# Hybrid decoder step: the last two prompt tiles' search moved into the block of the sample step

## The reference

```python
rel = relu(einsum('bthd,bsd->bths', iq, ik_all))      # 8 indexer heads of 64
score = einsum('bths,bth->bts', rel, iw)              # one score per query and key
score = where(k_pos <= q_pos, score, -inf)
_, sel = top_k(score, 256)
k_sel, v_sel = gather_kv(sel)                         # sample: from paged caches
p = softmax(q . k_sel * HEAD_DIM**-0.5 + rel_bias[bucket(q_pos - sel)])
o = p . v_sel
```

## Time and profile before

| | us |
|---|---|
| median of 3 runs | 4306.71 (4305.11 to 4307.8) |
| the profiled execution | 4302.77 |
| its span | 4301.3 |
| TensorE busy, share of the span | 3842.4, 89% |
| VectorE busy | 2194.8, 51% |
| ScalarE busy | 1531.6, 36% |
| GpSimd busy | 652.2, 15% |
| channels, first to last stores | about 205 to 1227 |
| block "step" | 1230 to about 1733 |

### The profile page before, as it was taken

How to read it: one execution, slowest core, us unless ns; L and a number is a source line. 1 busy time by engine, 2 the same in 40 slices (tenths; PEclk the granted TensorE clock), 3 DMA queues, 4 the chain that set the end, 5 groups by cost and what they waited for, 6 DMA issues and landing times. The chain is left out here.

```text
span 4301.3 us, 51935 instructions
## 1 busy us (share of the span) xinstructions
PE 3842.4 (89%) x19810; PEld 3139.1 (73%) x19882; DVE 2194.8 (51%) x4365; ACT 1531.6 (36%) x2446; POOL 652.2 (15%) x531
## 2 busy tenths in 40 slices
PE   7998887798859877888898879999999999989999
PEld 4554454455438556787887878899999999967877
DVE  6648988988963486343444333444434444430200
ACT  2135555665635334333333332322222222221211
POOL 0000000000000003322233210011111111133433
PEclk9999998999979669899999889999999999999999
DMA  3342222121142201111111124211211112163433
GB/s 113 94 99 56 73 49 61 46 63 39 47 145 94 80 9 45 32 37 28 48 36 45 33 78 132 79 40 40 59 39 55 44 39 59 47 227 108 137 114 107
DMA packets 287498, 298.52 MB, mean 69 GB/s; under 512 B 33871, under 2 KB 231375, under 8 KB 282410
## 3 DMA queue, kind: packets, MB, share of 16 engines
q1 hardware_dynamic: 264798, 250.51, 20.5%
q10 hardware_dynamic: 20400, 24.54, 1.7%
q0 software_dynamic: 2112, 20.97, 1.3%
HBM read 202.15 MB, written 94.10 MB: 69 GB/s over the span
## 5 line engine op out<-in xcount | busy, mean ns | idle before, releaser
L538 PE MATMUL chan_p_g<-ht,w_chan 128*128 128x412 f32 (+1 forms) x1760 | 677.2, 528 | 53.7 <-ACT chan_flat L586 33.6
L974 PE MATMUL up_p_g<-ht_high,up_wh 128*128 128x412 f32 (+1 forms) x1720 | 602.8, 350 | 0.0
L974 PE MATMUL up_p_g<-ht_high,up_wl 128*128 128x412 f32 (+1 forms) x1720 | 600.7, 349 | 0.0
L974 PE MATMUL up_p_g<-ht_low,up_wh 128*128 128x412 f32 (+1 forms) x1720 | 600.6, 349 | 0.0
L538 PEld LDWEIGHTS chan_p_g<-ht,w_chan 128*128 128x128 f32 x1760 | 341.4, 197 | 300.7 <-issue 233.5
L995 ACT ACTIVATE up_pre<-up_p_g 128x412 f32<-128x412 f32 (+1 forms) x220 | 113.2, 515 | 737.8 <-PE up_p_g L974 727.1
L1379 ACT ACTIVATE chan_signed<-chan_sc,chan_trial 128x512 bf16<-128x512 f32 (+6 forms) x224 | 304.9, 1361 | 148.4 <-DVE chan_trial L1434 127.7
L1059 DVE TENSOR_SCALAR up_acc<-up_pre,up_taps 128x2048 f32<-128x2048 f32 x44 | 59.3, 1347 | 557.8 <-ACT up_pre L995 557.8
L974 PEld LDWEIGHTS up_p_g<-ht_high,up_wh 128*128 128x128 f32 x1720 | 323.5, 188 | 1.1
L974 PEld LDWEIGHTS up_p_g<-ht_low,up_wh 128*128 128x128 f32 x1720 | 323.4, 188 | 1.2
L974 PEld LDWEIGHTS up_p_g<-ht_high,up_wl 128*128 128x128 f32 x1720 | 323.2, 188 | 0.5
(11 more groups left out here) (570 smaller groups left out, 7034.2 us busy)
## 6 DMA issues: line engine op xcount, KB each, us to landing
down_a<-scratch_act SPq DMA_DIRECT2D x88, 512.0 KB, 3.7
scratch_act<-up_acc SPq DMA_DIRECT2D x22, 1028.0 KB, 5.3
up_w<-in_w_up SPq DMA_DIRECT2D x44, 512.0 KB, 7.1
chan_iq<-scratch_iq SPq DMA_DIRECT2D x28, 512.0 KB, 7.3
scratch_qkv<-chan_acc SPq DMA_DIRECT2D x12, 1028.0 KB, 4.6
keys_of_raw<-scratch_qkv SPq DMA_DIRECT2D x16, 768.0 KB, 5.3
w_chan<-in_w_in SPq DMA_DIRECT2D x22, 512.0 KB, 4.6
proj_x<-in_x_prompt SPq DMA_DIRECT2D x16, 512.0 KB, 3.9
```

Of the source, the lines that this page charges most:

```text
L538: last = pe.matmul(p_g[u % BANKS][:, 0:cols.stop - cols.start], weights[:, k, :], K.ht[:, k, cols], start=(k == 0), stop=(k == KD - 1))
L974: last = pe.matmul(out, wp[s][:, k, :], hp[:, k, cols], start=(k == 0 and m == 0), stop=(k == KD - 1 and m == 2))
```

## The change

`Select` makes the scores of all pairs but searches only the first six (`self.searched`); its total shrinks by the last pair's search and masks. The scores of tiles 14 and 15 stay in SBUF (`K.last_sc`, held on the right side of SBUF until the end of "step"). A new class `LastSearch` runs their search and masks in the block "step", beside the attention, with one weight of 2.0 a round and 3.0 a mask (total 70); each engine advances it before the sample. The sample's index pages come in halves of a page (8 gathers instead of 4, each half as large, with buffers half as large), and the table's entries are loaded and doubled in channels. Values are gathered into the keys' buffer. ScalarE waits for the last sample score ahead of the rule.

```diff
@@ channels: sync, then vector
+            for req in range(2):
+                sp.dma_start(K.pid[req * NPAGE:(req + 1) * NPAGE, :], K.page_table[req], allow_slow_non_contiguous=True).then_inc(s_pid, 16)
...
+            dve.wait_ge(s_pid, 32)
+            dve.tensor_scalar(K.page_half[:, :, 0], K.pid[:, :], 1, None, ALU.logical_shift_left).then_inc(s_half, 1)
+            dve.tensor_scalar(K.page_half[:, :, 1], K.pid[:, :], 1, 1, ALU.logical_shift_left, ALU.bitwise_or).then_inc(s_half, 1)
+            dve.wait_ge(s_half, 2)
@@ Select
-        self.sc = two("sc", [P, SEQ])
+        self.sc = K.last_sc
+        self.searched = self.pairs[:-1]
...
-        return score + sum(32 * self.w_step(p) for p in self.pairs) + sum(self.w_mask(t) for _, _, t in self.tiles())
+        return score + sum(32 * self.w_step(p) + self.w_mask(2 * p) + self.w_mask(2 * p + 1) for p in self.searched)
...
+            if p not in self.searched:
+                return
@@ class LastSearch
+    W_COUNT, W_TRIAL, W_MASK = 1.0, 1.0, 3.0
...
+    def scalar(self, act):
+        for m in range(32):
+            act.wait_ge(self.s_tried, m + 1)
+            act.activation(self.signed[:, 0:self.NB], self.sc[1][:, 0:self.NB], ACT.Sign, scale=-1.0,
+                           bias=self.trial[:, 1:2].bitcast(F32), accum_out=self.signs[:, :]).then_inc(self.s_signs, 1)
+            yield self.W_COUNT
+            yield self.W_TRIAL
...
+    def vector(self, dve):
...
+            dve.wait_ge(self.s_tried, m + 1)
+            last = dve.tensor_scalar(self.tie[:, 0:self.NA], self.sc[0][:, 0:self.NA], trial[:, 0:1].bitcast(F32), None,
+                                     ALU.is_ge, ALU.add, accum_out=count[:, 0:1])
...
+            step(dve.tensor_scalar(miss[:, 0:1], count[:, 0:1], float(NSEL), None, ALU.is_lt))
+            yield self.W_COUNT
+            dve.wait_ge(self.s_signs, m + 1)
+            step(dve.tensor_scalar(miss[:, 1:2], self.signs[:, :], float(self.NB - 2 * NSEL), None, ALU.is_gt))
...
+            yield self.W_TRIAL
...
+            step(dve.tensor_scalar(tie, s, level, None, ALU.is_gt, ALU.add, accum_out=count[:, b:b + 1]))
+            dve.tensor_scalar(count[:, b:b + 1], count[:, b:b + 1], -1.0, float(NSEL), ALU.mult, ALU.add)
+            step(dve.tensor_scalar(tie, s, level, None, ALU.is_equal))
+            step(dve.tensor_scalar(left, s, level, None, ALU.is_lt))
+            step(dve.tensor_tensor_scan(s, tie, tie, 0.0, ALU.add, ALU.bypass))
+            step(dve.scalar_tensor_tensor(out=tie, in0=s, scalar=count[:, b:b + 1], in1=tie, op0=ALU.is_gt, op1=ALU.mult))
+            dve.tensor_tensor(left, left, tie, ALU.add).then_inc(self.s_left, 1)
+            yield self.W_MASK
@@ Sample
-        self.pages = [c.sb(f"pages{b}", [P, PAGE // 2, P]) for b in range(2)]
+        self.pages = [c.sb(f"pages{b}", [P, PAGE // 4, P]) for b in range(2)]
...
-        self.kg, self.vg = c.sb("kg", [P, QUARTERS, PAIRS, KVH * HD]), c.sb("vg", [P, QUARTERS, PAIRS, KVH * HD])
+        self.kg = c.sb("kg", [P, QUARTERS, PAIRS, KVH * HD])
+        self.vg = self.kg
...
-        cache = self.ins["cache_idx_k"].rearrange("l n p d -> (l n) (p d)")
+        cache = self.ins["cache_idx_k"].rearrange("l n (h p) d -> (l n h) (p d)", h=2)
...
     def begin(self, pool):
-        pool.wait_ge(self.S["pid"], 32)
...
         act.wait_ge(S["load"], 48)
+        act.wait_ge(S["sum"], self.UNITS)
@@ alongside, and its calls on SP, ScalarE and VectorE
-def alongside(main, side):
+def alongside(main, *sides):
     for w in main:
-        side.spend(w)
-    side.rest()
+        for side in sides:
+            side.spend(w)
+    for side in sides:
+        side.rest()
...
-                alongside(att.vector(dve), beside(sample.vector(dve)))
+                alongside(att.vector(dve), searching(last.vector(dve)), beside(sample.vector(dve)))
```

More of the change, by code:

```diff
@@ L458, in channels @@
         s_taps, s_zero, s_step, s_state, s_past = (c.sem(n) for n in ("taps", "zero", "step", "state", "past"))
+        s_pid, s_half = c.sem("pid"), c.sem("half")
         s_held, s_iqst = c.sems("held"), c.sems("iqst", IQS)
@@ L1341, in finished @@
     def finished(self, sp):
-        sp.wait_ge(self.s_out, 32 * len(self.pairs))
+        sp.wait_ge(self.s_out, 32 * len(self.searched))
     def tensor(self, pe):
@@ L2419, in __init__ @@
         self.S = {n: c.sem(f"s_{n}") for n in (
-            "pid iq wd bd w wread turn copy score mul sum "
+            "iq wd bd w wread turn copy score mul sum "
             "load state diag gates sq ss inv eg rs columns read vnew osq turned apart upd usum oss oinv ors mixed stored "
@@ L2555, in gpsimd @@
             yield self.W_SCORE
-            i = u // self.PER + 2
-            if (u + 1) % self.PER == 0 and i < PAIRS:
+            i = u // self.EACH + 2
+            if (u + 1) % self.EACH == 0 and i < self.HALVES:
                 pool.wait_ge(S["turn"], u + 1)
@@ L2660, in score_tensor @@
                 for k in range(4):
-                    last = pe.transpose(bank[u % 2][:, k * P:(k + 1) * P], self.pages[i % 2][:, u % self.PER * 4 + k, :], K.ident[:, :])
+                    last = pe.transpose(bank[u % 2][:, k * P:(k + 1) * P], self.pages[i % 2][:, u % self.EACH * 4 + k, :], K.ident[:, :])
                 last.then_inc(S["turn"], 1)
@@ L3175, in heads @@
             att = Attention(c, K, EARLY)
+            last = LastSearch(c, K)
             sample = Sample(c, K, ins, outs, bank)
             beside = lambda stream: Beside(stream, sample.total(), att.total())
+            searching = lambda stream: Beside(stream, last.total(), att.total())
             block = open_block(nc, stack, c)
@@ L3182, in _ @@
                 gate.sync(sp)
-                alongside(att.sync(sp, {-1: (0, 1), 6: (2,), 20: (3,)}), beside(sample.sync(sp)))
+                alongside(att.sync(sp, {-1: (0, 1), 6: (2,), 20: (3,)}), searching(last.sync(sp)), beside(sample.sync(sp)))
+                last.finished(sp)
                 att.finished(sp)
@@ L3194, in _ @@
                 gate.scalar(act)
-                alongside(att.scalar(act), beside(sample.scalar(act)))
+                alongside(att.scalar(act), searching(last.scalar(act)), beside(sample.scalar(act)))
             @block.gpsimd
@@ L3281, in build @@
             constants(nc, K, ins["rel_bias"])
+            K.pid, K.page_half = keep("pid", [P, PAIRS], I32, mixer), keep("page_half", [P, PAIRS, 2], I32, mixer)
+            K.page_table = ins["page_table"].rearrange("(i q) c -> q c i", q=2)
             K.vlast = keep("vlast", [P, KVH * HD], F32, mixer)
@@ L3294, in build @@
                             ins["norm_mix"].rearrange("l d -> (l d)"), w_in, ins["k_norm"].rearrange("l d -> (l d)"), outs)
+                K.last_scores = held.enter_context(ExitStack())
+                K.last_sc = [K.last_scores.enter_context(nc.sbuf_tensor(f"last_sc{b}", [P, SEQ - P + b * P], F32, side="right")) for b in range(2)]
                 channels(nc, K, w_in, ins["gdn_conv_w"].rearrange("l j n -> (l j) n"),
```

75 lines of the change are left out of this document (67 added, 8 removed).

## The result

The changed kernel takes 4326.1 us (median of 19 runs) where the kernel before takes 4309.9 (19 runs): a ratio of 1.0025, 95% interval 1.0016 to 1.0034. I had forecast 4281, so the sign was wrong. The 19 executions of the changed kernel spread from 4304.4 to 4333.5, those of the kernel before from 4303.5 to 4320.9. The profiled execution of the changed kernel took 4306.2 us, span 4304.7; a second one took 4320 with a span of 4318.4. Both are used, because the difference between them is part of the answer.

What follows compares the result with a forecast made beforehand. VectorE was taken to bound channels' searches, TensorE its scores and "step"'s sample scores and rule, VectorE "step"'s slots. 69 us added in "step" less 95 saved in channels gave -26: 4281 us, own range 4262 to 4298, with rivals 4247 to 4322.

Steps and rivals of the forecast that it cites:

- Scores, 22 predicted: Sample scores in "step": 14.4 rounds at 1.5 us each lengthen them by 22 us (0 to 39).
- rival 1: "step": rounds run serially at 2.70 us, clock slips (7 us), 95 saved in channels; +15, 4322 us; chance 0.17.
- Channels, 95 predicted: Channels: the last search's 139 us leave, less 27 scores, 11 taps, 3 ScalarE, 3 tail; 95 us saved.
- taps, 11 us more: Channels: a larger share of the taps lies in VectorE-bound searches and masks of pairs 1 to 6, 11 us more.
- my lower bound: Channels: some 70 us saved if TensorE's idle time of the searches stayed whole beside its extra matmuls.
- rival 4: Channels: denser scores and searches keep TensorE's stops; 70 us saved, 69 added, 4306 us, no change; chance 0.15.
- Start, -4 predicted: Start of "step": gathers no longer wait for the page table and half the bytes suffice to begin; -4 us.
- The second mask, +17 predicted: End of "step": the second mask falls between the sample's maximum and its softmax, adding 17 us (5 to 18).
- Search, slots, rule: "step": rounds beside the sample's search add 15 us, beside the slots 13, beside the rule 4.
- Blocks behind, 0 predicted: Blocks after "step": unchanged, 0 us.
- rival 2: Sample scores and rule hide all their rounds and channels gains its 113 us; -72, 4235 us; chance 0.16.
- Rival 3: ScalarE in "step": two table loads of 1.28 us per round, 37 us; +11, 4318 us; chance 0.04.

Runs made afterwards that it cites:

- experiment 11: The changed kernel with only the second mask moved to 99.0% of the attention's work, rounds from the start: 0.9976 of the kernel before, median 4309.6 us.
- experiments 4 and 12: Experiment 4: the changed kernel with GpSimd's first page gathers held behind the sample's query loads, 4310.2 us, ratio 1.0005; experiment 12 has its own line.
- experiments 5 to 12: Variants of the changed kernel with rounds or masks moved, gathers held, or Sign or count narrowed: ratios 0.9922 to 0.9991 to the kernel before.
- experiment 2: The changed kernel without the 32 rounds and both masks of tiles 14 and 15 in "step": 4232.0 us, ratio 0.9812 to the kernel before.
- experiment 12: The changed kernel with rounds from 13%, second mask at 99.0% and page gathers behind the query loads: 4292.3 us, 0.9922 of the kernel before.

## Why the prediction was wrong

The mechanism that I forecast happened part by part; the balance came out at +3 and +17 us in the two profiles instead of -26. Two terms were sized wrong: the price of a round beside the scores, and the taps in channels. Taking the second profile, the miss is 43 us: channels 16, scores 19, start 4, end 6, blocks behind 4, less 6 where search, rule and rest were cheaper than I said.

- **Scores, 22 predicted, 30 to 41 found: the largest error.** The step that failed is the price "1.5 us a round", taken as constant and as a stop of TensorE alone. I had put the clock into rival 1 only, as a slip from 0.97 to 0.92 over the whole stretch. The stops were smaller than I said: TensorE's idle time rose by 11 to 12 us, 0.7 to 0.8 us a round. The rest, 18 and 30 us in the two profiles (45 in experiment 11's), is busy time for the same instructions, at a mean clock of 0.86 and 0.81 (0.75) instead of 0.95. TensorE comes out of the loads at 0.50, and with whole Signs from the first head step the 20 us pieces stay between 0.57 and 0.78 for 60 to 80 us. In the five profiles with such Signs and gathers not held, the first 20 us read 0.59 to 0.66; without them, with a narrow Sign or with late rounds they read 0.87 to 0.89. With late rounds the first Sign comes some 50 us into the scores, and the clock still slips behind it, and the price was 1.0, 1.6 and 2.0 us a round in three profiles.
- **Channels, 95 predicted, 79 to 82 found.** The term that failed is "taps, 11 us more". I spread the taps evenly over the weights. The rows show them elsewhere: before, 48.5 us of them lay in the searches and masks of pairs 1 to 6, after it 79.0, so 30 us more, and these stretches, at VectorE's pace, grew by 35 where I had 14 (11 and ScalarE's 3). The scores with the tail gave 26 us where I had 30, and the block had 4 us more behind the last search than the 139 that I counted. TensorE's idle time ahead of the scores, the condition of my lower bound and of rival 4, mostly stayed (78 of 92 us); it lies under VectorE's searches, whose idle time hardly grew (27.6 to 32.0 us).
- **Start, -4 predicted, 0 found.** I took the wait for the page table away and did not ask what the earlier gathers would stand ahead of: the mask, gain and query loads. Held back (experiments 4 and 12), the pages come 4 us earlier, and the time follows by 3 to 4 us at most, inside the intervals.
- **The second mask, +17 predicted, +23 found.** Place and length were right (1688.4 to 1705.3 in the changed kernel). TensorE stood for 15.4 us and then took 3.41 us for sixteen 128x2 products that took 1.84 us before the change. 12 of the 23 us go with the mask; a low clock stays without it, and I had no term for that.
- **Search, slots, rule: right** (11, 13, 3 found for 15, 13, 4), and the first mask was hidden as said. In experiments 5 to 12 the stretch in which it lies took 54 to 71 us instead of 46, for reasons that were not tested, so this part is shown for this order alone.
- **Blocks behind, 0 predicted, +4 found.** It is there without any search too (2573.0 us in experiment 2), so the rounds don't cause it. 3.5 of the 4.5 us lie in "mid" (823.0 and 826.5); with one profile of the kernel before, what does it is open.

Rival 1 ended on the right number, and that is luck in part. ScalarE does stop a TensorE without slack, and the clock slips; but the stops were under a third of its 2.70 us a round and the clock's part far over its 7 us, its step block grew by 110 us where 81 and 92 were found, and it had channels at 95. In rival 2 the sum goes by 108 us for channels where its words say 113; with 113 it is 4230. Rival 3 is dead: beside 32 Signs, ScalarE has no table load that the kernel before lacked, 2446 instructions in all.

The Trainium skill, page "TensorE: Matmul & The Clock Gate", section "A second HAM failure mode: psum-queue depth-cycling", tells of a kernel in which short idle times between groups of matmuls, from cycling through PSUM banks, make the clock swing between its two levels. The rows agree in part: busy for 87% of the first 20 us at 0.59 with Signs between the evacuations, 96% at 0.89 without. But in experiment 12 TensorE was busy for 99% of its first 20 us, without a Sign, at 0.60. I had not weighed it.

Why one program shows 190.8 or 201.9 us for the same stretch, and experiment 11's 218.8, is not settled. The clock differs and the work doesn't, but what tips it from one execution to the next no profile shows. That the Signs' stops lower the clock is argued from which profiles are low; no run changed the clock alone.

## What to carry to other kernels

Price a moved piece of work by the stretch it lands in and by when in it: here the dearest place was the one in which TensorE had just come out of idle, where work on the engine that feeds it was paid once for the stop (11 to 12 us) and again for the clock (18 to 45). When work leaves one block for another, ask what the rest of the block's work will now lie beside: 30 us of taps moved into the searches whose pace VectorE sets, where an even share had said 11. A mask or any other lump belongs behind the last step that another engine waits for; here the move of one 17 us lump by a few instructions was worth 12 to 17 us. And where the clock differs between executions of one kernel, one profile doesn't price a round: the same order gave 1.0, 1.6 and 2.0 us.

## What the runs showed of the hardware

- The granted clock in the first 20 us of the sample scores falls into two groups over the changed kernels whose gathers are not held, 0.59 to 0.66 and 0.87 to 0.89, and each goes with whether Signs of 2 us lie between ScalarE's evacuations. With held gathers it reads 0.59 with and 0.60 without. The 40 us behind them part all profiles: 0.70 to 0.73 with Signs of 2 us from the start, 1.00 without.
- With the page gathers issued first, the loads at the start of the block kept the DMA engines at a share of 0.81 (274 GB/s), and SP's issue of four small loads took 9.51 us; with the gathers behind them it took 2.68.
- GpSimd's issue of an indirect gather took 0.95 us, and 4.53 beside VectorE's scan of 1920 elements. The Trainium skill, page "SBUF — State Buffer", section "Who interferes with whom", says that GpSimd and VectorE share one pair of SBUF ports, that the lock on it is exclusive, and that a VectorE instruction with two SBUF inputs contends with a GpSimd instruction that reads SBUF. The scan reads its mask tile twice, and the rows agree in size: it took 4.16 us.
